# Two transformer blocks on one core: accumulators zeroed by ScalarE, one weight split moved up, rotation by DMA, retention values centred before their product

## The reference, cut to what matters

```
u = rms_norm(h); fq, fk, fv, f_logit, rq, rk, rv, rg = split(u @ w_in)
fox = forgetting_attention(fq, fk, fv, f_logit)          # 8 heads of 64, softmax
q, k = apply_rotary(rq), apply_rotary(rk) * 64**-0.5     # t1*c - t2*s , t1*s + t2*c
ret = chunkwise_retention(q, k, rv, log_gamma)           # 8 heads, linear in rv
ret = (ret - mean_head(ret)) * rsqrt(var_head(ret) + 1e-5)
h = h + concat(fox, silu(rg) * ret) @ w_out
a, g = split(rms_norm(h) @ w_up); h = h + (gelu(causal_conv(a)) * g) @ w_down
h = h + sigmoid(rms_norm(h) @ w_gate) * (p @ w_proj)
```

## Time and profile before

| | us |
|---|---|
| median of 3 runs (lowest, highest) | 1362.68 (1360.9, 1364.52) |
| the profiled execution's own time | 1362.74 |
| its span in the trace | 1361.0 |
| PE busy | 1319.0 (97%) |
| DVE busy | 916.1 (67%) |
| ACT busy | 667.0 (49%) |
| DMA, mean rate over the span | 169 GB/s |

### The profile page before, as it was taken

The page is one execution under the profiler, slowest core; times in us unless marked ns, Lnnn a source line. Parts: engine busy times, 40 slices in busy tenths (PEclk is TensorE's granted clock), DMA queues, the critical chain, the costliest instruction groups (busy, mean ns, idle before and its releaser), DMA issues.

```text
span 1361.0 us, 21812 instructions
## 1 busy us (share of the span) xinstructions
PE 1319.0 (97%) x8766; PEld 1185.1 (87%) x8766; DVE 916.1 (67%) x1091; ACT 667.0 (49%) x764; POOL 31.2 (2%) x52
## 2 busy tenths in 40 slices
PE   7999999999999999998999999999999999999997
PEld 7998888888977888887998989999989988999997
DVE  4647666566455766558566787777686758877775
ACT  5635444435464544445454644444555445544454
POOL 0000000000021000001000000000020000000000
PEclk9999999999999999999999999999999999999999
DMA  9634655554523555553543345555545424555520
GB/s 369 243 125 155 247 185 186 185 186 159 184 91 124 187 188 192 193 195 118 174 153 108 141 167 182 185 183 184 179 152 183 139 87 160 186 185 185 185 93 32
DMA packets 33490, 229.85 MB, mean 169 GB/s; under 512 B 3728, under 2 KB 3984, under 8 KB 6032
## 3 DMA queue, kind: packets, MB, share of 16 engines
q1 hardware_dynamic: 31536, 220.21, 46.1%
q10 hardware_dynamic: 1888, 8.68, 1.8%
HBM read 227.83 MB, written 1.05 MB: 168 GB/s over the span
## 4 chain that ended last, share of the span: by engine, by line
PE 85%; DVE 7%; ACT 4%; issue 2%; DMA 1%; SPq 0%; POOL 0%; DVEq 0%; ACTq 0%
PE ring L336 18%; PE ring L334 9%; PE ring L277 9%; PE ring L278 8%; PE ring L279 8%; PE acc L379 4%; PE acc L381 4%; PE acc L380 4%; PE acc L277 3%; PE acc L279 3%; PE acc L278 3%; DVE wlo L269 2%; ACT whi L261 2%; PE ring L379 1%; PE ring L380 1%
## 5 line engine op out<-in xcount | busy, mean ns | idle before, releaser
L269 DVE TENSOR_TENSOR wlo<-raw,whi 128x2048 fp32r<-128x2048 f32 x207 | 475.1, 2299 | 183.2 <-ACT whi L261 183.0
L261 ACT CAST whi<-raw 128x2048 fp32r<-128x2048 f32 x207 | 393.9, 1907 | 109.4 <-PE ring L279 48.5
L336 PE MATMUL ring<-xs,whi 128*128 128x512 f32 x1184 | 420.0, 398 | 0.0
L334 PE MATMUL ring<-xs,wlo 128*128 128x256 f32 x1184 | 333.2, 281 | 0.2
L336 PEld LDWEIGHTS ring<-xs,whi 128*128 128x128 f32 x1184 | 222.5, 188 | 53.4
L277 PE MATMUL ring<-xs,whi 128*128 128x256 f32 x832 | 242.2, 291 | 13.3 <-DVE wlo L1544 6.4
L278 PE MATMUL ring<-xs,whi 128*128 128x256 f32 x832 | 236.6, 284 | 0.0
L279 PE MATMUL ring<-xs,wlo 128*128 128x256 f32 x832 | 236.5, 284 | 0.0
L334 PEld LDWEIGHTS ring<-xs,wlo 128*128 128x128 f32 x1184 | 223.8, 189 | 2.1 <-DVE wlo L269 1.0
L277 PEld LDWEIGHTS ring<-xs,whi 128*128 128x128 f32 x832 | 160.7, 193 | 18.5 <-issue 7.4
L278 PEld LDWEIGHTS ring<-xs,whi 128*128 128x128 f32 x832 | 160.9, 193 | 1.1 <-issue 1.0
(11 more groups left out here) (267 smaller groups left out, 1723.5 us busy)
## 6 DMA issues: line engine op xcount, KB each, us to landing
raw<-wstream SPq DMA_DIRECT2D x207, 1024.0 KB, 4.9
sq<-lnp ACTq DMA_DIRECT2D x4, 1024.0 KB, 4.9
cst<-consts ACTq DMA_DIRECT2D x1, 1029.0 KB, 14.8
hT<-xT SPq DMA_DIRECT2D x4, 256.0 KB, 4.9
raw<-wstream SPq DMA_DIRECT2D x4, 256.0 KB, 5.9
hT<-xtok ACTq DMA_DIRECT2D x1, 1024.0 KB, 18.8
misc<-decay ACTq DMA_DIRECT2D x1, 1024.0 KB, 4.8
out<-y SPq DMA_DIRECT2D x4, 256.0 KB, 2.3
```

The source lines that it names most:

```text
L261: act.copy(whi[:, c % SPLIT, :], raw[:, c % RAW, :]).then_inc(hi_made, 1)
L269: dve.tensor_tensor(wlo[:, c % SPLIT, :], raw[:, c % RAW, :], whi[:, c % SPLIT, :].bitcast(f32), ALU.subtract).then_inc(lo_made, 1)
L334: pe.matmul(bank(b + t)[:, 0:256], wl[:, w], xhi[:, k, :], start=k == 0, stop=False, skip_group_check=True)
L336: mm = pe.matmul(bank(b + t), wh[:, w], xs[:, k, :, :].rearrange("p a s -> p (a s)"), start=False, stop=k == NT - 1, skip_group_check=True)
```

## The change

It has seven parts.

1. The four rotation products of a layer's queries and keys leave PE. ACT issues four DMAs each time instead, 32 partitions x 4 KB each, that copy the swapped half-heads from `qT` or `kT` into `gT[:, 0:4]`; the sign goes into the sine table, and the constant `perm` is dropped. DVE's `rotary` moves from steps 8 and 10 to 9 and 11.
2. The retention values are centred by head on DVE, ahead of `scaled(13)`: a reduction of 128x1024 and two operations of 128x512. The output's head means are then zero, so the copy, the mean matmuls and the subtraction go; ACT squares straight from PSUM, PE puts the variances into `acc` banks 0 and 1, DVE scales from `acc`.
3. In `ffn` ACT zeroes `acc`, by copying a zero block of the constants 16 times, in place of DVE's memset.
4. In `ffn` both splits of chunk c0 + 4 move ahead of the first GELU and gating. In the steps that follow the order is as before.
5. In the gated linear attention DVE splits chunk 5 ahead of the scans, and ACT's `gate_exp` moves from after chunk 4 to after chunk 5.
6. After the last layer norm's last turn, PE runs three more `busy` matmuls.
7. `squares_sum` goes ahead of `forget_fold` after input chunk 1.

```diff
@@ last_two (PE)
                 turn(n, 1, src)
+                if early is None:
+                    busy(ln_bank(n, 0, 0)[:, 0:256], 3)
@@ input products and retention (PE)
                     if j == 1:
+                        squares_sum(3 * L, acc[:, 7, :])
                         forget_fold()
-                        squares_sum(3 * L, acc[:, 7, :])
...
-                    if j in (8, 10):
-                        rotate((j - 8) // 2)
...
                         if i == 0:
+                            pe.wait_ge(r_col_copied, L + 1)
...
                         pe.wait_ge(r_m, RET_H * L + h + 2)
+                        if i == 1:
+                            pe.wait_ge(r_vc, L + 1)
-                for j in range(2):
-                    pe.wait_ge(r_c, 2 * L + j + 1)
-                    pe.matmul(acc_bank(2 + j), blk, yf[:, 1024 + j * 512:1536 + j * 512], start=True,
-                              stop=True).then_inc(r_mean, 1)
                 def variances():
                     for e in range(2):
                         pe.wait_ge(r_sq, 2 * L + e + 1)
-                        pe.matmul(acc_bank(2 + e), blk, sqf[:, e * 512:e * 512 + 512], start=True,
+                        pe.wait_ge(x_made, 4 * (X + 1) + e + 1)
+                        pe.matmul(acc_bank(e), blk, yf[:, 1024 + e * 512:1536 + e * 512], start=True,
                                   stop=True).then_inc(r_var, 1)
@@ ffn (ACT)
                 g_crossed(c0 + 1, 0)
+                split_hi(act, c0 + 2 + AHEAD)
+                act.copy(acc[:, :, :].rearrange("p t s -> p (t s)").rearrange("p (a b) -> p a b", b=128),
+                         wide(maskadd[:, 128:256], 16)).then_inc(acc_zero, 1)
                 gelu(0)
                 high(0)
                     for i in range(1, 3):
-                        split_hi(act, ca + AHEAD, m)
                         a_crossed(ca, i, m)
                         split_hi(act, ca + 1 + AHEAD, m)
                         gelu(i, m)
                         g_crossed(ca + 1, i, m)
                         split_hi(act, ca + 2 + AHEAD, m)
                         high(i, m)
+                        split_hi(act, ca + 3 + AHEAD, m)
@@ gated linear attention (ACT)
-            evacuate(C_GLA_IN, 12, gla_dest, {0: a1_copy, 2: gate_ln, 4: gate_exp, 7: keys_copied, 10: first_squares})
+            evacuate(C_GLA_IN, 12, gla_dest, {0: a1_copy, 2: gate_ln, 5: gate_exp, 7: keys_copied, 10: first_squares})
@@ input products and head norm (ACT)
+                def swapped(n):
+                    act.wait_ge(gemm_free, FREE[f"in{L}"] + 8 + 2 * n)
+                    if n:
+                        act.wait_ge(r_rdy, 2 * L + 1)
+                    for p in range(0, 128, 32):
+                        act.dma_start(gT[p:p + 32, 0:4, :], (kT if n else qT)[p ^ 32:(p ^ 32) + 32, 4:8, :]).then_inc(r_swap, 16)
+                    if j in (8, 10):
+                        swapped((j - 8) // 2)
                     act.wait_ge(r_o, RET_H * L + 4 * j + 4)
-                    act.copy(pair(y, 2 + j), pair(acc, 2 + j)).then_inc(r_c, 1)
-                for j in range(2):
-                    act.wait_ge(r_yc, 2 * L + j + 1)
-                    act.activation(pair(sq, j), pair(y, 2 + j), ACT.Square).then_inc(r_sq, 1)
+                    act.activation(pair(y, 2 + j), pair(acc, 2 + j), ACT.Square).then_inc(r_sq, 1)
@@ ffn (DVE)
                 conv(0)
-                zero_acc(rs_made, 3 * L + 2)
+                split_lo(dve, c0 + 2 + AHEAD)
                 gated(c0 + 1, 0)
@@ gated linear attention (DVE)
             own.sync(dve.tensor_tensor(yf[:, 0:1024], yf[:, 0:1024], sqf[:, 0:1024], ALU.subtract))
+            split_lo(dve, 3 + AHEAD)
-            for c in (3, 4, 5):
+            for c in (4, 5):
                 split_lo(dve, c + AHEAD)
@@ input products, retention, head norm (DVE)
+                def centre_values():
+                    dve.wait_ge(gemm_free, FREE[f"in{L}"] + 12)
+                    by_head = v[:, :, 512:1024].rearrange("p t (h d) -> p t h d", d=64)
+                    dve.tensor_reduce(v_sum[:, :, :], by_head, mybir.AxisListType.X, ALU.add).then_inc(r_vs, 1)
+                    dve.wait_ge(r_vs, L + 1)
+                    for t in range(2):
+                        ins = dve.scalar_tensor_tensor(by_head[:, t], v_sum[:, t, :].unsqueeze(2).to_broadcast([128, RET_H, 64]),
+                                                       -1 / 64, by_head[:, t], ALU.mult, ALU.add)
+                    ins.then_inc(r_vc, 1)
                 def rotary(n):
-                    dve.wait_ge(r_rot, 2 * L + n + 1)
+                    dve.wait_ge(r_swap, 64 * (2 * L + n + 1))
-                    own.sync(dve.tensor_tensor(turned, acc[:, 4:8, :], wide(sinT, 4), ALU.mult))
+                    own.sync(dve.tensor_tensor(turned, turned, wide(sinT, 4), ALU.mult))
                     elif j >= 12:
+                        if j == 13:
+                            centre_values()
                         dve.wait_ge(r_rdy, 2 * L + 2)
-                    if j in (8, 10):
-                        rotary((j - 8) // 2)
+                    if j in (9, 11):
+                        rotary((j - 9) // 2)
-                for j in range(2):
-                    dve.wait_ge(r_mean, 2 * L + j + 1)
-                    dve.scalar_tensor_tensor(pair(y, 2 + j), pair(acc, 2 + j), -1 / 64, pair(y, 2 + j), ALU.mult,
-                                             ALU.add).then_inc(r_yc, 1)
-                    own.sync(dve.tensor_tensor(t, t, r, ALU.mult))
+                    own.sync(dve.tensor_tensor(t, acc_bank(2 + j), r, ALU.mult))
```

More of the change, by code:

```diff
@@ L50 @@
 NPV = 126 + 8 * FT
-CONST = dict(ident=0, ones=128, blk=384, tri=512, neg=640, perm=768, scan=896, mask=1152, cos=1536, sin=1792, eps=2048, fold=2050)
-NCONST = 2058
+CONST = dict(ident=0, ones=128, blk=384, tri=512, neg=640, scan=768, mask=1024, cos=1408, sin=1664, eps=1920, fold=1922)
+NCONST = 1930
 def build_program(nc, xT, xtok, lnp, wstream, wa1, wa2, wf, fbias, pT, params, consts, decay, out):
@@ L90, in build_program @@
         ln_st = sb("ln_st", [128, 2, 5])
+        v_sum = sb("v_sum", [128, 2, RET_H])
         stat = sb("stat", [128, 4, 8])
@@ L99, in par @@
             return pv[:, PV[name] + i:PV[name] + i + 1]
-        ident, blk, tri, neg, perm = (const(n, 128) for n in ("ident", "blk", "tri", "neg", "perm"))
+        ident, blk, tri, neg = (const(n, 128) for n in ("ident", "blk", "tri", "neg"))
         ones = const("ones", 128)
@@ L176, in build_program @@
             sem("fox_" + n) for n in ("log", "logit", "lnf", "cum", "z", "mx", "e", "p", "td", "tc", "o"))
-        r_rot, r_rdy, r_s, r_m, r_o, r_c, r_mean, r_yc, r_sq, r_var, r_rs = (
-            sem("ret_" + n) for n in ("rot", "rdy", "s", "m", "o", "c", "mean", "yc", "sq", "var", "rs"))
+        r_swap, r_rdy, r_s, r_m, r_o, r_vs, r_vc, r_sq, r_var, r_rs = (
+            sem("ret_" + n) for n in ("swap", "rdy", "s", "m", "o", "vs", "vc", "sq", "var", "rs"))
         def tok(t, half):
@@ L772, in scale_column @@
                     mm.then_inc(r_col_done, 1)
[L774 to L784, removed]
                 def fox_scores(p):
@@ L1047, in ffn @@
                         high(i, m)
-                split_hi(act, c0 + 3 * N_FF - 1 + AHEAD)
+                        split_hi(act, ca + 3 + AHEAD, m)
             def load_exp_ln():
@@ L1268, in _ @@
                     act.wait_ge(r_o, RET_H * L + 4 * j + 4)
-                    act.copy(pair(y, 2 + j), pair(acc, 2 + j)).then_inc(r_c, 1)
-                for j in range(2):
-                    act.wait_ge(r_yc, 2 * L + j + 1)
-                    act.activation(pair(sq, j), pair(y, 2 + j), ACT.Square).then_inc(r_sq, 1)
+                    act.activation(pair(y, 2 + j), pair(acc, 2 + j), ACT.Square).then_inc(r_sq, 1)
                 for j in range(2):
                     act.wait_ge(r_var, 2 * L + j + 1)
-                    power(rs[:, j * 512:j * 512 + 512], acc_bank(2 + j), 1 / 64, GN_EPS).then_inc(r_rs, 1)
+                    power(rs[:, j * 512:j * 512 + 512], acc_bank(j), 1 / 64, GN_EPS).then_inc(r_rs, 1)
                 split_hi(act, C_OUT[L] + 1 + AHEAD)
@@ L1321, in ahead @@
                     split_lo(dve, c + j + AHEAD)
-            def zero_acc(s, n):
-                dve.wait_ge(s, n)
-                dve.memset(acc[:, :, :], 0.0).then_inc(acc_zero, 1)
             def layer_norm(n, X, last=False):
@@ L1530, in ffn @@
                         ca = c0 + 3 * i - 1
-                        split_lo(dve, ca + AHEAD, m)
                         a_part(ca, i, m)
@@ L1537, in ffn @@
                         low(i, m)
-                split_lo(dve, c0 + 3 * N_FF - 1 + AHEAD)
+                        split_lo(dve, ca + 3 + AHEAD, m)
             for q in range(4):
@@ L1776, in _ @@
                 x_low(X + 1, lambda j: pair(acc, j), [1])
-                for j in range(2):
-                    dve.wait_ge(r_mean, 2 * L + j + 1)
```

(9 more changed lines are left out.)

## The result

The changed kernel takes **1342.1 us** (median of 4 runs, 1340.98 to 1343.15) beside 1362.39 us for the kernel before (4 runs, 1360.9 to 1364.52): a ratio of 0.985, 95% interval 0.9838 to 0.9862, so 20.3 us faster. The profiled execution of it took 1343.15 us, with a span of 1341.4. The forecast was 1342.3 us, and a gain.

The account below looks back on a forecast made before the run. PE, busy 97% of the span, was taken as the bound, so only its matmuls and waits count. From 1362.74 us, -6.8 - 3.4 + 1.0 - 8.0 - 1.4 - 1.45 - 0.4 = -20.4 gave 1342.3 us, range 1338 to 1352.

Parts of the forecast that it names:

- 1, rotations: Retention's queries and keys: four rotations taken off PE, 1.7 us each, all of it PE time: -6.8 us.
- 2, mean matmuls: Retention output: mean matmuls and the slow first matmul behind them go, 1.7 us, twice: -3.4 us.
- 2, centring late: Retention scores: centring on DVE makes scaled(13) late, 0.5 us in each layer: +1.0 us; bounds nothing and 3.1 a layer.
- 3 and 4: Feed-forward's first down product: 3.1 us idle and 1.6 of clock gained, 0.7 new wait; 4.0 a layer: -8.0 us.
- 5: Gated linear attention: PE's 1.32 us wait for chunk 5's split goes, with a 0.1 slow restart: -1.4 us.
- 6: First input chunk after the 2.01 us wait at 633.54: busy matmuls hold the clock, by judgement: -1.45 us.
- Swaps: Half-head DMAs ahead of DVE's rotary: costed at nothing, unless they land more than 5.7 us after the last issue.
- C: Rival at DVE's rotary, four times: swapped halves land late; 1379 us at a landing of 14.8; chance 0.06.
- Granted clock 1.00 throughout after the start: Sign of being right, for the whole kernel: PE's clock never falls to 0.50 once past the start.
- B: Rival: DVE late in more places, 2 us a layer more at scores and feed-forward's lower bound; 1350 us; chance 0.16.
- D: Rival: clock stays low; busy matmuls and shortened feed-forward gap give nothing back, 1.45 + 2 x 1.6 us; 1347; chance 0.08.
- E: Rival: more than summed, no new waits at scores or feed-forward, 1.0 + 1.4 us more gain; 1340 us; chance 0.10.

Follow-up runs that it names:

- all nine runs: Changed kernel, unaltered: its first four runs and five later ones, 1340.88 to 1343.16 us, median 1341.24.
- part 1 alone: Kernel before with only the rotation rows by DMA and rotary at chunks 9 and 11: 1355.48 us, ratio 0.9943.
- +0.6 (moved): Changed kernel with the centring moved from chunk 13 to chunk 11, ahead of the weights' split there: 1340.27 us, ratio 0.9839.
- -2.8 (undone): Changed kernel with copy, mean matmuls and subtraction back and no centring of the values: 1344.28 us, ratio 0.9865.
- -8.4 (undone): Changed kernel with DVE zeroing the accumulators and chunk c0+4's splits late again, both together: 1349.36 us, ratio 0.9901.
- -1.55 (undone): Changed kernel with the gate's exponential and chunk 5's split in their old places: 1342.42 us, ratio 0.9854.
- 0 in one execution: Changed kernel with the three more busy matmuls taken away: 1343.13 us, ratio 0.9849.

## Why the prediction was right

The forecast was 0.2 us off the first median and 1.1 off that of all nine runs, by which the gain is 21.2 us (1362.46 to 1341.24). Its steps, beside what the timelines and the parts undone show:

| step | forecast | seen | by experiment |
|---|---|---|---|
| 1, rotations | -6.8 | -6.9 | -7.0 (alone) |
| 2, mean matmuls | -3.4 | -3.4 | |
| 2, centring late | +1.0 | +0.6 | +0.6 (moved) |
| 2, net | -2.4 | -2.8 | -2.8 (undone) |
| 3 and 4 | -8.0 | -8.5 | -8.4 (undone) |
| 5 | -1.4 | -1.55 | -1.55 (undone) |
| 6 | -1.45 | -1.5 | 0 in one execution; 1 on average is an estimate from two falls in three |
| 7 | -0.4 | -0.4 | not tried |
| sum | -20.4 | -21.6 | |

- The rotations and means came out at their pitch because PE waited for nothing around them: a matmul taken from a full PE is worth all of it. The mean matmuls' second-order price, the slow first matmul behind them, was real too (0.69 again when they came back).
- *Centring.* The mechanism held, with `scaled(13)` late and the scores queued behind it. The forecast of 0.5 a layer is 0.57 of wait; what it missed is that the wait of 0.38 for the first value pair is then no longer there in full, which leaves 0.31. Of the inputs, three operations at 2.6 us took 2.5.
- *Feed-forward.* Forecast 3.1 us of idle, 1.6 of clock, 0.7 of new wait; seen 3.2, 1.35 in the down product itself, and 0.54, which makes 4.0. Of the other 0.2 of the 4.25 and 4.21, half lies at the join: from the last start of the second chunk's product to that of the down product it is 3.61 us before (789.92 to 793.53) and 0.28 after, 3.33 less and not 3.22. The other half lies in the two chunks' product behind the new wait, 11.31 us before (800.88 to 812.19) and 11.21 after (790.95 to 802.16). ACT's zeroing at the cast's price (1.91) took 1.88.
- *Swaps.* The last issue was forecast to end 4.5 us after chunk 11 starts, and it ended 4.35 after (709.54 to 713.89). The four issues took 2.45 us instead of 1.6 (0.5 to 0.6 each and not 0.36), but they begin beside the last exponential. The cover for the landing was put at 5.7 us, and is 6.6 for the keys and 5.9 for the queries; the longest landing seen is 5.0. So C had a real cause and too little of it. The landing was put at 2.6 us after the last issue, and was 1.8 in 51 groups of 52. The Trainium skill (SBUF, Door 1: The DMA port swizzle) says that 32 partitions in a row reach 8 of the 16 ports. The 1.2 us that the prediction made of it did not come. It had taken the four transfers as one of 512 KB behind the last issue; in the traces each lands 2.2 to 2.5 us after its own issue began (the late one aside), about 0.65 after the one before it. No run here moved the same rows in another shape, so they show nothing for or against the 8 ports.
- *Part 6* was called a judgement, and the term is the weakest: the -1.5 was seen in one pair of profiles and the fall that it removes is a matter of chance.
- "Granted clock 1.00 throughout after the start" was wrong: it fell at 318 us, where nothing was changed. That (0.3) and the fall at 18 with the rest of the start (1.7) are the 2 us between the terms' sum (-21.6) and the difference of the two spans (-19.6). The sum was too small by 1.2, and two of the first four runs of the changed kernel lie 2 us up (three of all nine), which made up for it: that the forecast came within 0.2 us is luck.
- B came as two waits of half a microsecond, as costed; D and E did not come.

## What to carry to other kernels

Where PE is 97% busy and its waits are few and long, cost each edit at the timeline: the matmuls removed at their pitch, the wait at its length plus what the lower clock costs behind it, and the next thing that is late on the engine that was relieved. Put added vector work where that engine's timeline shows an idle stretch, and not just ahead of its reader: the same 2.5 us of centring cost 0.6 us in one place and nothing in the other. In a pipelined loop look at the last group on its own, since there nothing hides the chain.

## What the runs showed of the hardware that was not expected

- **The clock's fall is not a fixed function of the wait.** At the places that the runs touch it fell after six of six waits of 3.13 to 3.23 us, after five of seven of 1.99 to 2.06, after one of 1.69 and neither of two of 1.75, and never after the 0.71 ahead of chunk 0 at 634 us. At the start of the program, at 17 us, it fell at waits of 1.76, 1.80 and 1.99 us, and not at 2.08 and 2.25, nor at nine of 0.46 to 1.69. At 316 to 318 us, with the same waits of 0.86 and 0.73 in each profile, it fell in five of fourteen. A fall costs about 1.5 us where nothing waits behind it; at 318 us only 0.3 of it is left, since a wait of 0.94 behind it goes. The changed kernel's scatter of 2 us would then be mostly the fall at 18, as its two profiled executions have it; the other seven runs have only a mean clock.
- **Low for twice as long**, once: beside the 3.21 us wait of L = 1 with part 1 alone it was 0.50 for 6.8 us instead of 3.4 (1145.0 to 1151.8; PE's wait ended at 1145.66). Windows of that run:

```profile
1145.00:1147.00 2.00, 1.34 (x6) 1.34 (x7) 1.90 (x3) 0.47 (x1) 0.00 (x0) 0.50 0.31 45
1147.00:1149.00 2.00, 2.00 (x11) 2.00 (x11) 1.62 (x4) 0.00 (x0) 0.00 (x0) 0.50 0.77 315
1149.00:1151.00 2.00, 2.00 (x12) 2.00 (x11) 1.86 (x3) 0.95 (x2) 0.00 (x0) 0.50 0.39 164
```

- **Landings hardly scatter, but one came late.** Four transfers of 128 KB were through 1.76 to 1.87 us after the last issue in 51 groups of 52, and 5.0 us after it in one. That one belongs to the only two groups that were issued while a 1 MB chunk of weights was in flight; why it was late and the other not stays open. A cover of 2 us would have done in all the others.
- **ScalarE zeroes PSUM as fast as it casts to SBUF**: 1.88 us for 128x2048, beside 1.76 for DVE's memset and 1.91 for the cast. A reduction by head over 128x1024 takes 1.21 us, as the rotary's operations of that size do.
